# An eighth place for 2 MB weight tiles, and a new order of the places, in a two-layer mixture-of-experts encoder

## The reference, cut to what matters

```python
for l in range(DEPTH):                                   # DEPTH = 2
    h = rms_norm(x, mix_norm_g[l])
    aq, ak, av, bq, bk, bv, cq, ckv, ckr, gates = split(h @ w_in[l])     # w_in: 1024 x 6816
    ...three attention branches, gated, then @ w_out[l]
    x = x + cross_attention(rms_norm(x), rms_norm(mem), ...)
    # experts: w1, w3 are 1024 x 512, w2 is 512 x 1024, 32 of each: 2 MB each, 201 MB a layer
    x = x + sum over a token's experts e of gate * (silu(h2 @ w1[e]) * (h2 @ w3[e])) @ w2[e]
return rms_norm(x, final_norm_g)
```

## Time and profile before

| | us |
|---|---|
| median of 3 runs (1585.85 to 1589.2) | 1587.27 |
| the profiled execution: its time | 1589.12 |
| its span in the profile | 1587.2 |
| TensorE busy (share of the span) | 1322.3 (83%) |
| VectorE busy | 622.0 (39%) |
| ScalarE busy | 301.8 (19%) |
| bytes moved by DMA | 502.31 MB, mean 316 GB/s |

### The profile page before, as it was taken

The page is one execution under the profiler, slowest core; times in us unless marked ns, Lnnn a source line. Parts: engine busy times, 40 slices in busy tenths (PEclk is TensorE's granted clock), DMA queues, the critical chain, the costliest instruction groups (busy, mean ns, idle before and its releaser), DMA issues.

```text
span 1587.2 us, 17941 instructions
## 1 busy us (share of the span) xinstructions
PE 1322.3 (83%) x7334; PEld 677.1 (43%) x7334; DVE 622.0 (39%) x1218; ACT 301.8 (19%) x748; POOL 21.7 (1%) x36
## 2 busy tenths in 40 slices
PE   8999999999657677678699999999986666767666
PEld 7986544463212133234179764445632211312212
DVE  5777676353122121121165866663531121121121
ACT  2235422251000001000032453212400000000002
POOL 2000000000000000000000000000000000000000
PEclk9999999999878788888799999999998888888888
DMA  9742236979999999999896323477899999999995
GB/s 302 227 163 80 73 113 235 350 251 403 423 428 429 428 401 429 429 428 428 361 297 191 122 80 119 172 263 272 297 422 426 428 428 427 402 428 428 426 427 227
DMA packets 105096, 502.31 MB, mean 316 GB/s; under 512 B 7217, under 2 KB 44145, under 8 KB 75185
## 3 DMA queue, kind: packets, MB, share of 16 engines
q1 hardware_dynamic: 102288, 496.50, 79.0%
q10 hardware_dynamic: 1888, 4.19, 0.7%
q0 software_dynamic: 832, 0.38, 0.3%
HBM read 500.00 MB, written 1.05 MB: 316 GB/s over the span
## 4 chain that ended last, share of the span: by engine, by line
PE 68%; DMA 26%; DVE 2%; issue 2%; ACT 2%; SPq 0%; DVEq 0%; ACTq 0%
DMA ring<-in_w_dram 22%; PE banks L2805 13%; PE banks L2510 9%; PE banks L2415 6%; PE banks L2890 6%; PE banks L2565 5%; PE banks L3002 3%; DMA shared<-in_w_dram 3%; PE banks L2307 3%; PE banks L2826 3%; PE banks L2408 3%; PE banks L2750 2%; PE banks L2859 1%; PE banks L2908 1%; PE banks L2676 1%
## 5 line engine op out<-in xcount | busy, mean ns | idle before, releaser
L2805 PE MATMUL banks<-ring,v 128*32 128x512 f32 x1312 | 255.1, 719 | 118.2 <-DMA ring<-in_w_dram 114.0
L2805 PEld LDWEIGHTS banks<-ring,v 128*32 128x32 f32 x1312 | 57.4, 129 | 284.1 <-DMA ring<-in_w_dram 159.9
L2890 PE MATMUL banks<-ring,probT 128*32 128x512 f32 x544 | 107.6, 741 | 39.4 <-DMA ring<-in_w_dram 33.6
L2805 PE MATMUL banks<-shared,v 128*32 128x512 f32 x224 | 122.0, 700 | 19.7 <-DMA shared<-in_w_dram 18.0
L1903 DVE COPY q<-banks 128x512 f32<-128x512 f32 x16 | 11.1, 692 | 241.5 <-PE banks L2890 159.6
L1899 DVE TENSOR_TENSOR q<-banks,q 128x512 f32<-128x512 f32 x16 | 11.1, 692 | 204.9 <-PE banks L2805 174.9
L2826 PE MATMUL banks<-ring,v 128*32 128x512 f32 x352 | 56.4, 669 | 19.5 <-DMA ring<-in_w_dram 16.2
L1892 DVE TENSOR_SCALAR q<-q 128x512 f32<-128x512 f32 x16 | 6.8, 427 | 165.2 <-ACT q L1136 165.2
L2750 PE MATMUL banks<-v,h 128*128 128x128 f32 x448 | 59.2, 295 | 12.4 <-issue 12.4
L2890 PEld LDWEIGHTS banks<-ring,probT 128*32 128x32 f32 x544 | 24.4, 132 | 102.1 <-DMA ring<-in_w_dram 47.5
L2750 PEld LDWEIGHTS banks<-v,h 128*128 128x128 f32 x448 | 56.5, 209 | 24.1 <-issue 24.1
(11 more groups left out here) (430 smaller groups left out, 2080.1 us busy)
## 6 DMA issues: line engine op xcount, KB each, us to landing
ring<-in_w_dram SPq DMA_DIRECT2D x116, 2048.0 KB, 18.6
ring<-in_w_dram SPq DMA_DIRECT2D x74, 1024.0 KB, 14.0
ring<-in_w_in_dram SPq DMA_DIRECT2D x52, 1024.0 KB, 7.8
shared<-in_w_dram SPq DMA_DIRECT2D x20, 2048.0 KB, 18.3
ring<-in_w_branch_dram SPq DMA_DIRECT2D x12, 1024.0 KB, 6.0
shared<-in_w_dram SPq DMA_DIRECT2D x12, 1024.0 KB, 9.8
ring<-in_w_out_dram SPq DMA_DIRECT2D x8, 1024.0 KB, 13.9
ring<-in_w_dram SPq DMA_DIRECT2D x12, 512.0 KB, 9.4
```

The source lines that it names most:

```text
L2805: last = nc.tensor.matmul(bank[2 + m][e * CAP:(e + 1) * CAP, :], xt[:, k, e * CAP:(e + 1) * CAP], ws[e][:, k * 512:(k + 1) * 512], start=k ...
L2890: last = nc.tensor.matmul(bank[6 + half][e * CAP:(e + 1) * CAP, :], hiddenT[:, k, e * CAP:(e + 1) * CAP], ws[e][:, k * D + half * 512:k * ...
```

## The change

It makes `gain`, `oa`, `prob` and `probT` views of one contiguous buffer, `pair_low`, whose first 16 KB of each partition are an eighth place, "low"; the old place in `shared` is called "high". The order of the places is new, tile n goes to place n mod 8, and `wait_place_free` (unchanged text) thus lets tile n go when the stage of tile n-8 is consumed. What used these buffers during the expert part moves: `hiddenT` to the second half of `probT`, the junk of `mem_squares` to `wide` (or `hT` in layer 0) with a wait between its two halves, the last norm's weights to `q0`. The first two tiles of w_in of layer 1 wait for the last group's w3 instead of for the counter that its w2 moves.

```diff
-PAIR_SLOTS = (None, 8, 10, 0, 2, 4, 6)
-PAIR_AFTER = (KD - 1, 2 * KD - 1, 2 * KD + 3, 2 * KD + 3, PER_QUAD - 1, PER_QUAD - 1, PER_QUAD - 1)
+PAIR_SLOTS = ("low", "high", 0, 10, 8, 2, 4, 6)
+PAIR_AFTER = (KD - 1, KD - 1, 2 * KD + 3, 2 * KD + 3, 2 * KD - 1, PER_QUAD - 1, PER_QUAD - 1, PER_QUAD - 1)
+PAIR_BESIDE = {"low": 7, "high": 4}
...
-        gain = sb("gain", [P, D])
+        pair_low = sb("pair_low", [P, 2 * SLOT + SEQ * 2])
+        gain = pair_low[:, 0:D]
...
-        prob = sb("prob", [P, NPB, 2, SEQ])
-        probT = sb("probT", [P, 2, 2, TT, P])
-        oa = sb("oa", [P, 4, SEQ])
+        pair_beside = {"low": pair_low[:, 0:2 * SLOT], "high": shared[:, SEQ + SLOT:]}
+        oa = pair_low[:, D:2 * D].rearrange("p (c n) -> p c n", n=SEQ)
+        prob = pair_low[:, 2 * D:2 * D + NPB * 2 * SEQ].rearrange("p (b a n) -> p b a n", b=NPB, a=2)
+        probT = pair_low[:, 2 * D + NPB * 2 * SEQ:].rearrange("p (b j c n) -> p b j c n", b=2, j=2, c=TT)
...
-        hiddenT = probT[:, 0, :, :, :].rearrange("p a b n -> p (a b) n")
+        hiddenT = probT[:, 1, :, :, :].rearrange("p a b n -> p (a b) n")
...
-                    sp.wait_ge(slot_free, l * PER_LAYER + (j + 1))
+                    if l > 0 and j < 2:
+                        sp.wait_ge(slot_free, done_at(l - 1, QUADS - 1, 2 * KD - 1))
+                    else:
+                        sp.wait_ge(slot_free, l * PER_LAYER + (j + 1))
...
-                    nc.scalar.activation(memjunk[t], memx[:, t, :], ACT.Square,
+                    if l > 0 and t > 0:
+                        act.wait_ge(mem_squared, (l + 1) * TT + t)
+                    nc.scalar.activation(wide_flat if l > 0 else hT_halves[t], memx[:, t, :], ACT.Square,
                                          accum_out=stat[:, 9 + t:10 + t]).then_inc(mem_squared, 1)
```

More of the change, by code:

```diff
@@ L390, in bass_hybrid_encoder @@
         memx_rows = q0[:, :, :].rearrange("p c n -> p (c n)").rearrange("p (t n k) -> p t n k", t=TT, k=KD)
-        memjunk = (gain[:, :], oa[:, :, :].rearrange("p c n -> p (c n)"))
+        wide_flat = wide[:, :, :].rearrange("p c n -> p (c n)")
+        hT_halves = [hT[:, 4 * t:4 * t + 4, :].rearrange("p c n -> p (c n)") for t in range(TT)]
+        end_gain = q0[:, :, :].rearrange("p c n -> p (c n)")[:, 0:D]
         landed = [sem(f"landed{i}") for i in range(RING)]
@@ L462, in slot_loads, with own_loads @@
                     sum(PAIR_SLOTS[n % PLACES] == s - 1 for n in range(HALVED, PAIRS)))
+        def own_loads(i):
+            return 2 if i < 2 or i in AGAIN_AT else len(extras[i])
         def extra_loads(i):
-            return 2 + (sum(PAIR_SLOTS[n % PLACES] is None for n in range(0 if i == AGAIN_AT[0] else HALVED, PAIRS))
-                        if i in AGAIN_AT else 0)
+            return own_loads(i) + sum(PAIR_BESIDE.get(PAIR_SLOTS[n % PLACES]) == i for n in range(PAIRS))
         def pair_no(q, j):
@@ L958, in _ @@
             plain(pool)
-            nc.gpsimd.dma_start(gain[0:1, :], final_norm_g.rearrange("(a n) -> a n", a=1)).then_inc(gain_in, 16)
+            nc.gpsimd.dma_start(end_gain[0:1, :], final_norm_g.rearrange("(a n) -> a n", a=1)).then_inc(gain_in, 16)
             pool.wait_ge(row_copied, DEPTH + 1)
@@ L962, in _ @@
                 wait_end_added(pool, last, 2 * t)
-                nc.gpsimd.tensor_tensor(h[:, t, 0:512], x[:, t, 0:512], gain[:, 0:512], ALU.mult).then_inc(end_gained, 1)
+                nc.gpsimd.tensor_tensor(h[:, t, 0:512], x[:, t, 0:512], end_gain[:, 0:512], ALU.mult).then_inc(end_gained, 1)
         @block.scalar
@@ L1145, in experts_round @@
                     act.wait_ge(row_made, DEPTH + 1)
[L1146 to L1147 removed]
+                    nc.scalar.activation(end_gain[:, 0:512], bank[0][:, :], ACT.Copy)
+                    nc.scalar.activation(end_gain[:, 512:1024], bank[1][:, :], ACT.Copy).then_inc(row_copied, 1)
                 act.wait_ge(S["y_made"], rd + 1)
@@ L1485, in end_half @@
                     dve.wait_ge(row_copied, DEPTH + 1)
-                    last = nc.vector.scalar_tensor_tensor(h[:, t, cols], x[:, t, cols], rstd(t), gain[:, cols],
+                    last = nc.vector.scalar_tensor_tensor(h[:, t, cols], x[:, t, cols], rstd(t), end_gain[:, cols],
                                                           ALU.mult, ALU.mult)
@@ L2778, in weights @@
                             i = AHEAD.index(j)
-                            pe.wait_ge(extra_in[i], 16 * (extras_in * extra_loads(i) + 1) if i < 2 or i in AGAIN_AT
-                                       else (extras_in * 16 + 16) * len(extras[i]))
+                            pe.wait_ge(extra_in[i], 16 * (extras_in * extra_loads(i) + len(extras[i])) if i not in (0, 1)
+                                       else extras_in * 32 + 16)
                         return lambda c: beside(i, c)
@@ L2838, in experts_round @@
                     pe.wait_ge(gain_in, 32)
-                    nc.tensor.matmul(bank[0][:, :], ones[0:1, :], gain[0:1, 0:512], start=True, stop=True)
-                    nc.tensor.matmul(bank[1][:, :], ones[0:1, :], gain[0:1, 512:1024], start=True, stop=True)\
+                    nc.tensor.matmul(bank[0][:, :], ones[0:1, :], end_gain[0:1, 0:512], start=True, stop=True)
+                    nc.tensor.matmul(bank[1][:, :], ones[0:1, :], end_gain[0:1, 512:1024], start=True, stop=True)\
                       .then_inc(row_made, 1)
```

14 lines of the change are left out of this document (6 added, 8 removed).

## The result

The changed kernel takes 1575.13 us (median of 4 runs, 1573.0 to 1575.46) where the kernel before takes 1586.56 us (1585.12 to 1589.2). The ratio is 0.9923, with a 95% interval of 0.9906 to 0.994. Timed once more it gave 1573.72 us and the same ratio, 0.9923 (0.9909 to 0.9937). The forecast was 1572.2 us, in a range of 1569.0 to 1579.5. The profiled execution took 1573.0 us, with a span of 1571.2 us, 16.0 less than before's 1587.2.

A forecast was written before the change was run, and what follows sets the result against it. The prediction took the DMA to bound the expert parts and TensorE layer 1's mixing part. 4.5 us at the check plus 10.6 at the layer ends, 15.1 off a median of 1587.27, gave 1572.2 us, range 1569 to 1579.5.

The forecast's parts named there:

- What bounds the kernel: Expert parts are bound by the DMA, layer 1's mixing part by TensorE; only four windows of low DMA rate matter.
- The layer ends: Group 7 of both layers: all w2 transfers queue behind w1, so the DMA doesn't stop; 5.2 + 5.4 = 10.6 us.
- The three parts of the sum: Layer ends, layers 0 and 1: w2 starts earlier, 2.9 and 2.0; last row's stop, 0.8 and 1.9; full clock, 1.5 each.
- the two bounds of the prediction: Gain at the layer ends: by TensorE 10.6 us, by the DMA's last landings 5.8 and 5.6 us (11.4).
- The check: Overflow branch before group 4: four w3 tiles queued cover w1's late product, closing gaps of 2.2 and 2.35 us, 4.5 together.
- The sum: Whole kernel: 4.5 us at the check plus 10.6 at the layer ends, 15.1 us off.
- w_in and the order: Layer 1's w_in issued behind w3, 0 to 0.5 us, worth 0 by itself; new place order, 0 us.
- Rival 1: Last group of each layer: the clock falls all the same, gain 4.5 + 7.6 = 12.1 us, 1575.2; 20%.
- Rival 2: Group 4: closing the check's gap doesn't pay, something between w3 and w2 is late next; 10.6 us alone, 1576.7; 9%.
- Rivals 3 and 4: 3: places don't do what they should, no change, 1587.3, 5%; 4: transfers in flight share the DMA, slower, 1592, 4%.

The follow-up runs named there:

- h_all: Changed kernel, but every fourth tile goes only when the stage of tile n-7 is consumed, as with seven places; 1586.11 us, ratio 1.0003.
- p_order: Changed kernel with places 8 and 0 swapped back, so w_in's first tiles wait for w2's first two second halves; 1573.64 us, ratio 0.9917.
- after_rep: The changed kernel profiled and timed once more, nothing edited; 1573.72 us, ratio 0.9923.
- h_check: Changed kernel, but in group 4 of both layers the fourth w3 tile waits for w1 as before; 1575.31 us, ratio 0.993.
- g_nocheck: Changed kernel without the overflow flag's reading, the branch before group 4 and the rounds for overflowing experts; 1573.36 us, ratio 0.9916.
- u_win_old: Changed kernel, but w_in's first two tiles of layer 1 wait for their old counter, w2's first half; 1572.45 us, ratio 0.9914.
- m_rows: Changed kernel, but the second halves of all four last-group w2 matrices come in 12 transfers instead of 6; 1573.8 us, ratio 0.992.

## Why the prediction was right, point by point

**What bounds the kernel.** Right: closing the four windows of the earlier trace rows shortened the kernel; h_all, which differs from the changed kernel only in how long every fourth tile waits, has the dips back and is at 1.0003.

**The layer ends, 5.2 + 5.4 = 10.6 us.** Right in mechanism and size. C to D went from 24.77 to 20.17 us and from 26.17 to 20.01, which is 4.6 and 6.2, 10.8 together; over all kernels with the gap (means 25.9 and 25.0) against those without (20.1 and 20.2, the 21.55 left out and p_order's 20.87 counted) it is 5.7 and 4.8. The times give 11.1. The 21.55 is left out for the late landing told above; with it the first difference is 5.5. The three parts of the sum can be read one by one, before against after_rep, layers 0 and 1. w2's product starts 2.35 and 2.59 us earlier behind C (expected 2.9 and 2.0). The product up to the last row's stop takes 2.1 and 2.3 us less (expected 1.5 from the clock; the rest is not accounted for). The stop ahead of the last row falls by 0.1 and 1.3 us (expected 0.8 and 1.9): it is still 0.65 and 0.58 us (0.88 in the first profile's layer 0), where I expected under 0.5, since by the DMA's side the last row simply lands at 20.0 us. So each part was off by 0.5 to 0.8 us, and that they add up so well is in part luck. TensorE and the DMA came out nearly level, as the two bounds of the prediction, 10.6 and 11.4, had it.

**The check, 4.5 us.** The mechanism was right and the size off; this is the mis-sized term. It measured 2.0 + 1.0 = 3.0 us between landmarks and 1.1 (at most 3) by the times. The prediction took the whole dip of the rate, 2.2 and 2.35 us, as time. The dips were real, but a rate counts all 16 engines and a landing only the last. In the kernel before, the 16 engines finish the first tile behind the gap 2.1 us late in the mean, in layer 0, and 2.3 in layer 1. The last engine finishes it only 0.5 and 0.1 us late, because it was 3.5 to 4.1 us behind the first when the gap came and still had work; behind the gap all are within 0.8 us. h_all and h_check have the same picture. Being in step again doesn't last: in each of these traces and layers a later tile lands 0.9 to 1.3 us late behind a packet of instructions, and that cost is paid a second time. In the changed kernel no gap closes the ranks, and most of the later packets delay no landing. From A to C the last engine is late by 3.3 and 3.0 us in all before, and by 1.5 to 2.1 in all kernels whose eighth place works at the check. These are readings of the traces; no run was made for them.

The same record answers, as far as the order of events can, what the 1.6 us are that A to C still has above 215.3. In the changed kernel the two stages across the check, A to w3 of group 4, take 594.06 - 553.59 = 40.47 us where two stages at the DMA's pace are 39.15, though the rate is 426 GB/s. In these 40.47 us one landing comes 6.01 us behind the one before it, while 15 of its 16 parts are done after 5.09, and a packet of instructions was begun 3.2 us ahead of it. g_nocheck has no loss there (596.20 - 557.05 = 39.15), but its w1 of group 5 takes 636.67 - 615.78 = 20.9 us: the first tile of that stage lands 6.21 us behind the one before, 15 of its 16 parts after 5.02, behind one packet at 619.35 us (window 619.3 to 620.5):

```profile
q8 instruction: 1, 0.02, 5.8%
```

The Trainium skill, "DMA: Bandwidth & Descriptors", section "Two DMAs through the same engine are not ordered", allows such a skew between engines; the traces agree, with 0.7 to 5.2 us between the first and the last of the 16, between A and C in all kernels.

**The sum.** 15.1 us predicted; 10.8 + 3.0 = 13.8 between landmarks (10.5 + 3.0 by the means), and 1586.5 x 0.0077 = 12.2 by the times (9.5 to 14.9 by the interval). The span fell by 16.0: 12.3 in the four stretches of the table, 1.4 ahead of A, and 2.3 because the profile of before took longer in layer 1's routing, between D and the next A. The last two have nothing to do with the change. Windows of the kernel before:

```profile
1130.00:1135.00 5.00, 5.00 (x34) 4.06 (x33) 3.96 (x34) 4.06 (x8) 0.00 (x0) 0.82 1.02 394
1135.00:1140.00 5.00, 5.00 (x25) 5.00 (x25) 3.36 (x22) 1.98 (x8) 0.00 (x0) 0.50 0.96 345
```

and of the same work in the changed kernel:

```profile
1125.00:1130.00 5.00, 4.81 (x35) 3.84 (x33) 4.68 (x37) 4.59 (x7) 0.00 (x0) 1.00 1.03 394
1130.00:1135.00 5.00, 4.99 (x48) 3.00 (x51) 2.22 (x13) 2.10 (x10) 0.00 (x0) 1.00 0.94 358
```

The granted clock fell to 0.50 there with TensorE busy throughout. From D to w2 of group 3 in layer 1 it was 531.74 us before, and 529.2 to 529.8 in every other kernel of either kind in the table.

**w_in and the order.** Worth 0 within what can be measured, as p_order and u_win_old show. On the old counter w_in would go at 786.73 us, still some 4 us ahead of the latest issue that was in time. TensorE's waits from 800 to 1130 us in the changed kernel are as in the earlier trace rows, none of them for the DMA:

```profile
PE banks L3053 <- DVE pair_low L1869: 0.9, 1, 0.9
```

**The rivals.** Rival 1 (clock): the time, 1575.13, is the one it named, 1575.2, but its reason isn't there, the clock is 1.00 in both last groups. Rival 2 (the check's gap doesn't pay): the times alone don't exclude it, 1.1 us with an interval from nothing; the landings do, 3.0 us of 4.5, and its reason, something late between w3 and w2 of group 4, isn't there, as the rate stays at 424 to 428 GB/s. Rivals 3 and 4 didn't come.

## What to carry to other kernels

Where a phase is bound by the DMA, look for the short windows in which its rate falls, and count how many bytes are queued when the slowest consumer comes free: one place more was worth 0.8% because at two kinds of points the queue was shorter (14.7 and 7.4 us) than the consumer's delay. Don't take a dip of the rate at its full length: the rate is a sum over the DMA's engines, a landing waits for the last of them, and that one may have had work through most of the dip. Measure from landing to landing, over whole stages. Behind the last transfer of a phase, cut the tail so that less work follows it, and check that the smaller rows don't cost as much in the landing.

## What the runs showed of the hardware that I had not expected

- One 16 KB packet of instructions can make a tile land 1.0 to 1.3 us late (read from the order of events) when the DMA is busy without a break, while the GB/s of the window show nothing.
- SP's issues can be slow. The chain of the changed kernel has those of w2's rows at 0.43 us and then at 3.26 and 3.63 us; before, with fewer transfers queued ahead, the same four took 0.45 to 0.65 us. That the queue's depth is the cause is likely and not tested:

```profile
760.68 0.43 SPq L837
761.11 0.04 issue
761.15 3.26 SPq L837
764.41 0.04 issue
764.45 3.63 SPq L837
```

  In the changed kernel nobody waits for SP then. In m_rows the twelve issues fill 21.7 us.
- The granted clock can fall to 0.50 under a busy TensorE in one execution and not in the next: for 6.8 us in the profile of before, which cost 2.3 us.
- Start to A varies from 553.6 to 557.1 us among kernels with nearly the same code up to there, so spans of single profiles tell less than stretches do.
